# Decay exponents of a chunked scan: fetched back as broadcast rows instead of TensorE products, and zeros stored beside the input stage

## The reference, cut to what matters

```
def step(state, inp):                       # one chunk
    xdt_c, dA_c, B_c, C_c = inp
    acum = jnp.cumsum(dA_c, axis=1)
    seg = acum[:, :, None] - acum[:, None, :]
    decay = jnp.exp(jnp.where(causal[None, :, :, None, None], seg, -jnp.inf))
    cb = jnp.einsum('blgn,bsgn->blsg', C_c, B_c)
    y_diag = jnp.einsum('blsg,blsgr,bsgrp->blgrp', cb, decay, xdt_c)
    y_off = jnp.einsum('blgn,bgrpn,blgr->blgrp', C_c, state, jnp.exp(acum))
    to_end = jnp.exp(acum[:, -1:] - acum)
    new_state = (state * jnp.exp(acum[:, -1])[..., None, None]
                 + jnp.einsum('bsgn,bsgr,bsgrp->bgrpn', B_c, to_end, xdt_c))
```

## Time and profile before

| what | value |
|---|---|
| median of 3 runs | 1900.31 us (1895.75 to 1904.19) |
| profiled execution, its own time | 1903.38 us |
| its span from first to last instruction | 1901.6 us |
| mean granted TensorE clock | 0.974 |
| PE busy | 1790.3 us (94%) |
| DVE / ACT / POOL busy | 916.4 (48%) / 718.1 (38%) / 698.8 us (37%) |
| DMA moved | 409.50 MB, mean 215 GB/s |

### The profile page before, as it was taken

The page is one execution under the profiler, slowest core; times in us unless marked ns, Lnnn a source line. Parts: engine busy times, 40 slices in busy tenths (PEclk is TensorE's granted clock), DMA queues, the critical chain, the costliest instruction groups (busy, mean ns, idle before and its releaser), DMA issues. The chain is left out here.

```text
span 1901.6 us, 29246 instructions
## 1 busy us (share of the span) xinstructions
PE 1790.3 (94%) x9708; PEld 1241.6 (65%) x9708; DVE 916.4 (48%) x2041; ACT 718.1 (38%) x1854; POOL 698.8 (37%) x799
## 2 busy tenths in 40 slices
PE   6999999988999799999999999999998999999994
PEld 3444444677444588888888546468545888888882
DVE  5687744577213464343434530147454644343337
ACT  0443200455112454545454310134244444444441
POOL 1333300155112485555554330300134955545540
PEclk9989999999999899999999999999998999999997
DMA  9865567721202799999996612200227999999964
GB/s 338 292 229 195 191 213 239 260 87 45 83 11 93 277 325 348 338 333 318 333 323 162 234 60 89 101 1 1 73 86 286 316 335 327 327 327 348 336 171 163
DMA packets 170255, 409.50 MB, mean 215 GB/s; under 512 B 37652, under 2 KB 45188, under 8 KB 170164
## 3 DMA queue, kind: packets, MB, share of 16 engines
q1 hardware_dynamic: 132724, 337.77, 49.3%
q0 software_dynamic: 37440, 70.56, 14.9%
HBM read 394.23 MB, written 79.75 MB: 249 GB/s over the span
## 5 line engine op out<-in xcount | busy, mean ns | idle before, releaser
L1336 ACT ACTIVATE arena<-psum,lncol 128x128 f32<-128x128 f32 x1024 | 371.6, 468 | 417.3 <-PE psum L834 417.2
L856 PE MATMUL psum<-arena 128*128 128x128 f32 x4096 | 502.3, 278 | 0.0
L856 PEld LDWEIGHTS psum<-arena 128*128 128x128 f32 x4096 | 479.5, 193 | 1.0 <-issue 1.0
L1871 DVE COPY arena<-arena 128x1 f32 (+1 forms) x128 | 19.7, 154 | 463.7 <-PE psum L856 463.7
L868 PE MATMUL psum<-arena 128*128 128x512 f32 x512 | 241.1, 593 | 0.7 <-DVE arena L1889 0.7
L2243 POOL DMA_INDIRECT expert_sum<-arena,idx x124 | 198.9, 1604 | 40.7 <-issue 40.4
L1889 DVE SCALAR_TENSOR_TENSOR arena<-psum,arena 128x512 f32<-128x512 f32 x256 | 181.9, 743 | 15.1 <-PE psum L868 14.8
L834 PEld LDWEIGHTS psum<-ident,arena 128*128 128x128 f32 x1024 | 122.0, 143 | 74.8 <-issue 64.3
L2214 POOL TENSOR_TENSOR passed<-ones 128x1 f32<-128x1 f32 x252 | 50.2, 199 | 302.9 <-DVE arena L1889 291.2
L2230 POOL DMA_INDIRECT arena<-h_rows,idx x128 | 139.7, 1091 | 19.3 <-issue 4.1
L834 PE MATMUL psum<-ident,arena 128*128 128x128 f32 x1024 | 136.9, 277 | 8.7 <-DMA arena<-h_rows,idx 7.7
(11 more groups left out here) (285 smaller groups left out, 2335.6 us busy)
## 6 DMA issues: line engine op xcount, KB each, us to landing
arena<-in_moe_w_dram SPq DMA_DIRECT2D x384, 512.0 KB, 6.1
arena<-in_ada_w_dram SPq DMA_DIRECT2D x38, 1024.0 KB, 5.2
arena<-in_ssm_w_in_dram SPq DMA_DIRECT2D x9, 2048.0 KB, 11.3
arena<-in_ada_w_dram SPq DMA_DIRECT2D x5, 2048.0 KB, 10.1
arena<-in_ssm_w_out_dram SPq DMA_DIRECT2D x4, 2048.0 KB, 9.0
expert_sum<-arena SPq DMA_DIRECT2D x4, 2048.0 KB, 15.1
arena<-expert_sum SPq DMA_DIRECT2D x16, 512.0 KB, 5.3
arena<-in_kv_ada_w_dram SPq DMA_DIRECT2D x4, 1024.0 KB, 5.2
```

The source lines that it names most:

```text
L856: mm = pe.matmul(psum[:, b, 0:P], w[:, k, :], xeT[u % 2][:, k, :], start=(k == 0), stop=(k == KC - 1))
L1336: ins = act.activation(xeT[u % 2][:, k, :], psum[:, b, P * j:P * j + P], ACT.Identity, scale=h_scale(l, k), bias=h_shift(l, k))
```

## The change

Three things, of which the first is the main one.

1. The exponents are no longer products. Once, behind z tile 0, PE forms the cumulated steps in both layouts (`sum_steps`: four 32x128 products and four 128x32), ACT moves them out (`acumT`, `acum`), and SP stores `acumT` to DRAM. For each step q SP fetches the 8 rows of its heads, 4 KB, broadcast to all 128 partitions, into `decay[q % 2]` (512 KB written, `load_acum`); the fetch of q waits until both `mixm` halves of q - 2 are done. ACT then takes, in place, relu(acum - row) for each head (eight of 128x128) and exp(-that) in two halves. `stepm` and L668 are gone, and ACT waits on itself (`act_step`) between the two.
2. The zeros go out in four stores spread over the input stage, behind the blocks n = 3 and 5 and z blocks 0 and 1, instead of at the scan's start.
3. `ALONE_AT` changes, so the last ada sum closes behind z tile 14 rather than 15; `decay` now lies over the ada weights' buffer, and its first fetch waits for that sum.

```
-        decay = [view(124 + 2 * i, 4 * P) for i in range(2)]
+        decay = [view(124 + 8 * i, GH, P) for i in range(2)]
+        acumT = view(136, S)
+        acum = view(138, T, HEADS)
-        stepm = [view(132 + 0.5 * i, P) for i in range(8)]
...
-        ALONE_AT = (1, 3, 4, 6, 7, 9, 11, 12, 14, 15)
+        ALONE_AT = (1, 2, 4, 5, 7, 8, 10, 11, 13, 14)
...
+            def sum_steps():
+                pe.wait_ge(dA_ready, 1)
+                ps = claim(6)
+                for ch in range(T):
+                    mm = pe.matmul(ps[0:HEADS, TILES[ch]], dA[:, ch, :], upper[:, :], start=True, stop=True)
+                fill(mm, 6, "acumT")
+                ps = claim(7)
+                for ch in range(T):
+                    mm = pe.matmul(ps[:, HEADS * ch:HEADS * ch + HEADS], upper[:, :], dA[:, ch, :], start=True, stop=True)
+                fill(mm, 7, "acum")
...
-                for half in range(2):
-                    pe.wait_ge(stepm_ready, 2 * q + half + 1)
-                    ps = claim(1 + half)
-                    for j in range(4):
-                        mm = pe.matmul(ps[:, P * j:P * j + P], stepm[4 * half + j], upper[:, :], start=True, stop=True)
-                    fill(mm, 1 + half, ("seg", q, half))
...
+                until_drained(act, "acum")
+                act.wait_ge(acum_in[q % 2], 16 * (q // 2 + 1))
                 for half in range(2):
-                    ps = until_filled(act, ("seg", q, half))
-                    if q + 1 < NQ:
-                        segments(q + 1, half)
-                    if q:
-                        act.wait_ge(mixm_ready, 2 * (q - 1) + half + 1)
-                    act.activation(decay[half], ps, ACT.Exp).then_inc(drained[1 + half], 1)
+                    for j in range(4 * half, 4 * half + 4):
+                        h = GH * g + j
+                        ins = act.activation(decay[q % 2][:, j, :], decay[q % 2][:, j, :], ACT.Relu, scale=-1.0,
+                                             bias=acum[:, ch, h:h + 1])
+                    ins.then_inc(act_step, 1)
+                for half in range(2):
+                    part_ = decay[q % 2][:, 4 * half:4 * half + 4, :].rearrange("p h l -> p (h l)")
+                    act.wait_ge(act_step, 2 * q + half + 1)
+                    act.activation(part_, part_, ACT.Exp, scale=-1.0).then_inc(decay_ready, 1)
...
+                if n in (3, 5):
+                    store_zeros()
...
+                if n < 2:
+                    store_zeros()
+                if n == 2:
+                    until_drained(sp_, "acumT")
+                    sp_.dma_start(acum_dram.rearrange("(c h) p -> h c p", c=T),
+                                  acumT[0:HEADS, :].rearrange("h (c p) -> h c p", c=T)).then_inc(acum_out, 16)
+
+            def load_acum(q):
+                src = acum_dram[GH * q:GH * q + GH, :].rearrange("h p -> (h p)")
+                sp_.dma_start(decay[q % 2].rearrange("p h l -> p (h l)"), src.partition_broadcast(P)).then_inc(acum_in[q % 2], 16)
+            sp_.wait_ge(ada_summed[0], ADA_OF[0])
+            sp_.wait_ge(acum_out, 16)
+            for q in range(2):
+                load_acum(q)
...
+            def next_acum(q0, q1):
+                for q in range(q0, q1):
+                    sp_.wait_ge(mixm_ready, 2 * (q - 1))
+                    load_acum(q)
+            next_acum(2, 13)
```

More of the change, by code:

```diff
@@ L237, in trunk @@
         rows_dram = nc.dram_tensor("h2_rows", [S, D], F32, kind="Internal").ap()
+        acum_dram = nc.dram_tensor("acum_rows", [T * HEADS, P], F32, kind="Internal").ap()
         mod_dram = nc.dram_tensor("mod_rows", [112, P], F32, kind="Internal").ap()
@@ L275, in trunk @@
         pool_step = sem("pool_step")
-        vec_cols = sem("vec_cols")
         cond_ready = sem("cond_ready")
@@ L282, in trunk @@
         dA_ready = sem("dA_ready")
-        exps_ready = sem("exps_ready")
-        stepm_ready = sem("stepm_ready")
+        acum_out = sem("acum_out")
+        acum_in = [sem(f"acum_in{i}") for i in range(2)]
         xdt_ready = sem("xdt_ready")
@@ L634, in _ @@
                         fill(mm, b, ("z", kind[1], t))
+                        if (kind[1], t) == (0, 0):
+                            sum_steps()
                         for a in ada_beside_z(kind[1], t):
@@ L1238, in _ @@
                     for t in range(T):
+                        if (key[1], t) == (0, 1):
+                            ps = until_filled(act, "acumT")
+                            act.activation(acumT[0:HEADS, :], ps[0:HEADS, :], ACT.Copy).then_inc(drained[MARK["acumT"][0]], 1)
+                            ps = until_filled(act, "acum")
+                            act.activation(acum.rearrange("p a b -> p (a b)"), ps[:, 0:P], ACT.Copy
+                                           ).then_inc(drained[MARK["acum"][0]], 1)
                         move(("z", key[1], t), zs[:, t, 512 * key[1]:512 * key[1] + 512], ACT.Silu)
@@ L1243, in _ @@
             act.wait_ge(ada_summed[0], ADA_OF[0])
[L1245 to L1251, removed]
             def scan_exps(q):
@@ L1283, in move_y @@
                     ins.then_inc(drained[MARK[("yT", ch, g)][0]], 1)
-            for half in range(2):
-                segments(0, half)
             scan_exps(0)
@@ L1607, in scan_g @@
                 for half in range(2):
-                    until_drained(dve, ("seg", q, half))
+                    dve.wait_ge(decay_ready, 2 * q + half + 1)
                     if q:
@@ L1611, in scan_g @@
                     dve.tensor_tensor(mixm[half].rearrange("p (h l) -> p h l", h=4),
-                                      decay[half].rearrange("p (h l) -> p h l", h=4),
+                                      decay[q % 2][:, 4 * half:4 * half + 4, :],
                                       CBm[q % 2].unsqueeze(1).to_broadcast([P, 4, P]), ALU.mult).then_inc(mixm_ready, 1)
@@ L1642, in move_y @@
                     ins.then_inc(drained[MARK[("yT", ch, g)][0]], 1)
+            dve.wait_ge(acum_out, 16)
             scan_a(0)
@@ L2410, in _, with store_zeros @@
             stream(1)
+            sp_.wait_ge(zero_ready, 1)
+            stores = iter([(l, a) for l in range(2) for a in range(SUMS)])
+            def store_zeros():
+                l, a = next(stores)
+                sp_.dma_start(sum_dram[l][a].rearrange("(p a) (b c) -> p (a b) c", p=P, c=512),
+                              zero.unsqueeze(1).to_broadcast([P, S * D // 512 // P, 512])).then_inc(zeros_out, 16)
             for n in range(CT // 4):
@@ L2455, in _ @@
                 mod_col(SHIFT2, l, SH2)
-            sp_.wait_ge(zero_ready, 1)
-            for l in range(2):
-                for a in range(SUMS):
-                    sp_.dma_start(sum_dram[l][a].rearrange("(p a) (b c) -> p (a b) c", p=P, c=512),
-                                  zero.unsqueeze(1).to_broadcast([P, S * D // 512 // P, 512])).then_inc(zeros_out, 16)
+            def next_acum(q0, q1):
[3 more added lines that the diff above has]
+            next_acum(2, 13)
             until_filled(sp_, ("yT", 1, GROUPS - 1))
@@ L2463, in _ @@
             sp_.dma_start(w_last, items[n_items0 - 1][1]).then_inc(last_in, 16)
+            next_acum(13, NQ)
             sp_.wait_ge(squared, NQ)
```

## The result

The changed kernel takes 1918.0 us in the median of 6 runs (1913.2 to 1919.4), beside 1898.2 us of the kernel before on the same chip, also of 6 runs: a ratio of 1.0092, with a 95% interval of 1.0076 to 1.0108 (the quotient of the two medians is 1.0105, so the interval may be somewhat too narrow). It is slower by 0.9%, and its median lies 1 us above the top of the predicted range. Its profiled execution took 1919.0 us with a span of 1917.1 us, 15.5 us longer than the span before, at a mean granted clock of 0.954 instead of 0.974.

What follows compares the result with a forecast made beforehand. PE bounds most of the kernel; the scan's chunks 0 to 2 follow a DVE, POOL, PE loop, chunk 3 DVE. Work terms -2.8 plus clock +10.4 gave +7.6 on 1903.4: 1911.0 us profiled, median 1908, range 1893 to 1917.

Steps and rivals of the forecast that it cites:

- The mechanism: In the scan, removed products lengthen PE's waits for POOL, its clock falls, and ordinary steps get slower; forecast chance 0.55.
- the fetch does not set the pace: Rival in the scan: fetch landing in 7.8 us slows chunk 3, +5.2 us over the forecast, median 1913.1; chance 0.13.
- The term of the clock: Ordinary steps of chunks 0 to 2: seven slow steps, +12.3 us, less 1.9 for the old stretch, +10.4.
- the price of a slow step: Extra time of a scan step at the lower clock: 1.75 us, bounds 1.2 and 2.3.
- The old slow stretch's -1.9: The slow stretch already in the scan before, 1.2 plus 0.7 us in two steps, no longer counted as extra.
- The zeros: Input stage: the store ahead of z tile 8's loads adds one wait reaching PE; +0.5 us, bounds 0 and 4.
- The sums of the steps: Input stage: `sum_steps` costs its own PE time, 1.0 plus 0.5; +1.5 us, bounds 1.0 and 2.6.
- Steps behind a turned chunk: Scan steps 4 to 5, 8 to 9, 12 to 13: L668 on the path; -3.5 us, bounds -1.7 and -5.8.
- Head of the scan: Earlier table load, and the exponential's second half right behind the first; -1 us, bounds +1.5 and -2.5.
- The fetch: Scan: landing taken as 4.2 us, 10.2 us per two steps, fits everywhere, in chunk 3 barely; 0 us.
- The ada sum: Moving it takes DVE's last addition out of the way of the scan's first transpose; -0.3 us.
- a clock that stays up: Rival in the scan: the longer waits bring no lower clock; median 1895.6 us; chance 0.27.

Runs made afterwards that it cites:

- a1: The changed kernel with eight dummy 128x128 products in every scan step, where the exponents' products stood; 1900.8 us, ratio 1.0011 to the kernel before.
- b3: The changed kernel with dummies in scan steps except behind turned chunks, all zeros behind x, B, C blocks, two dummies in three ada waits; 1887.3 us, 0.9934.
- a4: The changed kernel with all four zero stores ahead of the z blocks, behind blocks n = 2, 3, 4, 5; 1911.5 us, ratio 1.0049.
- b1: The changed kernel with dummies in scan steps except behind turned chunks, and all zeros behind the x, B, C blocks; 1894.7 us, ratio 0.9975.
- b3_again: The kernel of b3 unchanged, measured a second time with twelve runs for four; 1892.0 us, ratio 0.9956.
- a3: The kernel before with only the zero stores at their new places and the moved ada sum; 1907.4 us, ratio 1.0041.
- b2: The kernel before with two dummy 128x512 products ahead of three ada sums of the x blocks; 1897.1 us, ratio 0.9993.

## Where the prediction was right, and where its size was off

**The mechanism was right.** Ordinary steps of chunk 1 are still 8.04 us where the clock is full (a1, b3), so the removed products were not on the path there; the clock fell, to 0.72 over the scan where 0.75 was named; the fetch does not set the pace. The chance of a slowdown by over 0.5% stood at 0.35 all the same, since the size was off. One part of the mechanism was not foreseen: the prediction looked at the waits for POOL alone, and three of the eight slow steps, 7.6 us, belong to the stretch that began behind PE's two shorter waits in the head of the scan.

**The term of the clock: +12.3 forecast, 17.5 measured in the same steps, 20 in the whole scan.** This is the term that was mis-sized, and in it the price of a slow step. Against b3_both, which has the same scan at the full clock and without dummies in the turned steps, the changed kernel's scan is 138.11 - 118.04 = 20.1 us longer. The eight slow steps together cost 17.5 us of it, and the last step, not in the count, another 1.5 (5.61 for 4.16 us). The price: 1.75 us was the middle between a fall that comes after L682 has begun and one before it. Behind the longest waits the clock has fallen before L689 starts, so both products are slow whole, 2.08 - 1.12 and 3.52 - 1.89, and a slow step costs 2.5 us, above the upper bound of 2.3 (three of the eight were slow only in part, so their mean is 2.2). The row of the single fall was the wrong neighbour, since its wait was half as long. The count: I took seven of nine, as a slow stretch shortens the next wait. It does, to 0.71 or 1.19 us, but the next step is slow nevertheless: from 368 to 399 us the clock is low without a break, from 416 to 436 over two steps. But a4, with the same scan, has six slow steps of 2.4 us in the mean, 14.5 together; so the count of seven was as good as these traces can tell, and the price is what failed. The old slow stretch's -1.9 was right: 42.11 - 40.24.

The Trainium skill says in "TensorE: Matmul & The Clock Gate", section "HAM oscillation — how this bites in real kernels", that a loop of short bursts of matmuls and waits can be slowed in each turn. The trace agrees in that eight of the ten ordinary steps between step 0 and step 12, and the last one, are slow; but from 368 to 399 us the clock did not rise between the turns.

**The zeros: +0.5 forecast, 3.6 measured** (a4's z blocks against those of after). The wait was named and looked for, and its bounds of 0 to 4 held it; but I priced one small wait and not the slow stretch behind it, which is half of the 3.6. That PE waits for DVE's ada sums in the z blocks stood among the signs of a wrong forecast, and it came. It is the same omission: a wait of PE was priced by its length alone.

**The sums of the steps: +1.5 forecast, 1.9 measured.** The passes of 128 columns take 243.83 - 242.84 = 1.0 as worked out; those of 32 columns take 0.9 instead of the 0.5 that I took.

**Steps behind a turned chunk: -3.5 forecast, -3.1 measured**, and -3.4 at the full clock (27.21 - 23.86, b3). a1 with its dummies gives 27.23, so here the products were on the path. The half taken for the first two holds: in b3 they gain 0.8 each, and the third 1.7.

**Head of the scan: -1 forecast, -1.8 measured.** The exponential is no sooner in itself, but its second half follows the first without triangles between:

```profile
362.80 2.44 ACT L1270 ACTIVATE arena<-arena 128x128 f32<-128x128 f32 x8
...
365.14 1.14 ACT L1276 ACTIVATE arena<-arena 128x512 f32<-128x512 f32 x2
```

**The fetch: 0 forecast, 0 measured,** with 3.6 us in the median where 4.2 was taken:

```profile
DMA to landing us min/median/max: 3.5/3.6/5.0
```

The sign I had named for it was wrong: ACT's relus do have a DMA as releaser of seven waits, without harm, since DVE has work until the exponentials come. A wait of an engine says nothing until someone waits for that engine.

**The ada sum: -0.3 forecast,** not seen apart. What this list leaves unassigned in the profiled spans is small (0.6 us in the z blocks); the -2.9 us of the x blocks I take for no effect of the change.

**The chances.** The forecast's own range let a slow step cost at most 2.3 us, and nine of those, 1900.3 - 2.8 - 1.9 + 20.7 = 1916.3, already fill it. The bounds of the other terms, which it was said to hold, were not added, so that its top could not hold eight of 2.2 and a slow last step beside 3.6 for the zeros. The 0.27 for a clock that stays up leaned on "seven of eight waits of 1.4 to 1.8 us did nothing". That was misread: three of the eight were 0.5 to 1.1 us, and of the three of 1.76 us one was followed by a fall. Without the x blocks the two profiled spans differ by 12.3 + 5.9 + 0.2 = 18.4 us, and the medians by 19.9. "Within 0.5%" got the largest chance because +7.6 us lies just inside it, while its largest term stood between a lower bound from a milder case and an upper bound that was too low.

## What to carry to other kernels

Work of TensorE that ends in a wait costs nothing there and may be what keeps its clock up: before it is removed, add its time to the wait and ask what the clock did behind the longest waits of the trace, and price a fall at the whole slow products behind it, in most turns of the loop. Waits elsewhere that the same work filled count too, as those in the head of this scan. A load that is new on a path needs its queue free of all that could stand there for nothing before, and stores moved out of its way have to be priced at the loads that they are moved in front of, with the slow stretch of the clock that a wait of PE brings behind it. Where such work must go, dummy products in the waits can be worth it: here 16.6 us of the scan, and with the stores placed well and dummies left out where PE is on the path, a kernel 0.25% (b1) to 0.4% (b3_again) faster than before, with intervals that overlap.

## What was not expected of the hardware

The clock's answer to a wait is not sharp: of 13 waits of about 1.8 us in a loop of otherwise the same work 3 were followed by the lower clock, of 4 of about 2.7 us 2 were, and of 10 from 2.83 us on all were. Two waits of 1.15 and 1.49 us close together, with PE busy for 3.36 us of the 6 around them, were followed by the longest slow stretch of all. And a slow stretch outlived the step that began it, with waits as short as 0.71 and 1.19 us inside it, so that the step times of one kernel switch between 8.04 and 10.56 us, or 6.8 and 9.33. Products of one column behind a wait, 8 of which keep PE busy for 0.95 us, did not hold the clock up at 304 us in a3, and in b2 it fell behind 1.84 us of them at 84 us with no wait ahead. A broadcast fetch of 512 KB landed in 3.6 us in the median (3.5 to 5.0) with its queue free, and the same fetch was 24 us late for DVE behind four stores of 2 MB each.
